# Two transformer-like blocks on one core: the x spill cut into eight pieces, and the order of the opening's chunks changed

## The reference, cut to what matters

```python
shift, scale, gate = split(silu(c) @ ada_w[l] + ada_b[l], 3)        # 2048 x 6144
shift_c, scale_c, gate_c = split(silu(c_ctx) @ ada_w[l] + ada_b[l], 3)
h  = rmsnorm(x,  norm_g[l]) * (1 + scale)   + shift
hc = rmsnorm(xc, norm_g[l]) * (1 + scale_c) + shift_c
q, k, v, up, uf, g = split_proj(h @ w_in[l])                        # 2048 x 4608
kc, vc, ...        = split_proj(hc @ w_in[l])
att = latent_attention(q, k, v, kc, vc)
x_new = x + gate * merge_branches(att, up, uf, g, ...) 
```

## Time and profile before

| | us |
|---|---|
| median of 3 runs | 2350.74 (2350.19 to 2352.19) |
| profiled execution, its own time | 2353.96 |
| its span, first to last instruction | 2352.1 |
| TensorE busy | 2271.9 (97%) |
| VectorE busy | 1297.0 (55%) |
| ScalarE busy | 1040.3 (44%) |
| GpSimd busy | 266.7 (11%) |
| moved by DMA | 437.14 MB, mean 186 GB/s |

### The profile page before, as it was taken

The page is one execution under the profiler, slowest core; times in us unless marked ns, Lnnn a source line. Parts: engine busy times, 40 slices in busy tenths (PEclk is TensorE's granted clock), DMA queues, the critical chain, the costliest instruction groups (busy, mean ns, idle before and its releaser), DMA issues.

```text
span 2352.1 us, 30034 instructions
## 1 busy us (share of the span) xinstructions
PE 2271.9 (97%) x11859; PEld 1832.5 (78%) x11859; DVE 1297.0 (55%) x2046; ACT 1040.3 (44%) x1592; POOL 266.7 (11%) x326
## 2 busy tenths in 40 slices
PE   5989999999999989999999998999999999999998
PEld 2567777777777867678888887888888888888887
DVE  3333453442432364555777776677755777567764
ACT  2222333432321255445554565555544555345553
POOL 1001100000010122100020324111100111001111
PEclk8999999999999999999999998999999999999999
DMA  9874443345655475735566544565656565666653
GB/s 357 316 277 167 147 144 110 110 142 172 224 178 179 148 273 192 238 96 159 182 208 203 176 139 152 179 197 180 188 191 194 182 186 187 197 188 187 188 190 116
DMA packets 322428, 437.14 MB, mean 186 GB/s; under 512 B 13849, under 2 KB 220113, under 8 KB 321265
## 3 DMA queue, kind: packets, MB, share of 16 engines
q1 hardware_dynamic: 316800, 413.19, 54.2%
q0 software_dynamic: 3392, 16.90, 2.0%
q10 hardware_dynamic: 2096, 5.15, 0.6%
HBM read 428.89 MB, written 6.29 MB: 185 GB/s over the span
## 4 chain that ended last, share of the span: by engine, by line
PE 85%; DVE 5%; ACT 4%; DMA 3%; issue 2%; POOL 1%; SPq 0%; ACTq 0%; POOLq 0%
PE ps L1361 24%; PE ps L1362 12%; PE ps L1336 8%; PE ps L1338 8%; PE ps L1337 8%; PE ps L1356 5%; PE ps L1358 5%; PE ps L1357 5%; PE ps L1316 3%; ACT SPL L1567 2%; DVE SPL L1818 2%; DMA RAW<-in_w_in_dram 2%; PE ps L1410 1%; PE ps L1427 1%; DMA RAW<-in_ada_w_dram 1%
## 5 line engine op out<-in xcount | busy, mean ns | idle before, releaser
L1818 DVE TENSOR_TENSOR SPL<-RAW,SPL 128x1024 fp32r<-128x1024 f32 x592 | 752.6, 1276 | 637.9 <-ACT SPL L1567 635.3
L1361 PE MATMUL ps<-HS,SPL 128*128 128x512 f32 x2688 | 959.8, 401 | 10.4 <-DVE SPL L1818 7.5
L1567 ACT ACTIVATE SPL<-RAW 128x1024 fp32r<-128x1024 f32 x592 | 621.7, 1055 | 451.2 <-PE ps L1338 174.0
L1362 PE MATMUL ps<-HS,SPL 128*128 128x256 f32 x2688 | 756.6, 281 | 0.0
L1361 PEld LDWEIGHTS ps<-HS,SPL 128*128 128x128 f32 x2688 | 507.9, 189 | 136.1 <-DVE SPL L1818 5.3
L1362 PEld LDWEIGHTS ps<-HS,SPL 128*128 128x128 f32 x2688 | 511.0, 190 | 2.0 <-issue 1.7
L1336 PE MATMUL ps<-SPL,HS 128*128 128x512 f32 x960 | 396.6, 413 | 18.7 <-DVE HS L1867 6.6
L1338 PE MATMUL ps<-SPL,HS 128*128 128x512 f32 x960 | 379.2, 395 | 0.0
L1337 PE MATMUL ps<-SPL,HS 128*128 128x512 f32 x960 | 378.7, 394 | 0.0
L1336 PEld LDWEIGHTS ps<-SPL,HS 128*128 128x128 f32 x960 | 183.2, 191 | 83.0 <-issue 28.6
L1337 PEld LDWEIGHTS ps<-SPL,HS 128*128 128x128 f32 x960 | 183.4, 191 | 41.3 <-issue 5.3
(11 more groups left out here) (289 smaller groups left out, 1691.2 us busy)
## 6 DMA issues: line engine op xcount, KB each, us to landing
RAW<-in_w_in_dram SPq DMA_DIRECT2D x208, 512.0 KB, 5.7
RAW<-in_ada_w_dram SPq DMA_DIRECT2D x192, 512.0 KB, 5.0
RAW<-in_ffn_w_up_dram SPq DMA_DIRECT2D x192, 512.0 KB, 3.6
RAW<-in_w_out_dram SPq DMA_DIRECT2D x96, 512.0 KB, 4.7
RAW<-in_ffn_w_down_dram SPq DMA_DIRECT2D x96, 512.0 KB, 4.2
x_spill<-XT POOLq DMA_DIRECT2D x2, 2048.0 KB, 15.0
XT<-x_spill POOLq DMA_DIRECT2D x1, 4096.0 KB, 16.6
MM<-in_x_dram ACTq DMA_DIRECT2D x2, 1024.0 KB, 10.8
```

The costliest lines, as they stand in the source:

```text
L1361: mm(PS[b][:, :], wr, hh, start=k == 0, stop=False, skip_group_check=True)
L1362: m = mm(PS[b][:, 256:512], wl, hh[:, 0:256], start=False, stop=k == KT - 1, skip_group_check=True)
L1567: act(SPL[:, (n - 1) % NSPL, 0, :], raw_of(i), ACT.Copy).then_inc(s_hi, 1)
L1818: tt(w[:, 1, :], raw_of(s["i"]), w[:, 0, :].bitcast(F32), ALU.subtract).then_inc(s_lo, 1)
```

## The change

- The spill goes in eight DMAs of 512 KB (`PIECES` = 4 for each half), one behind each projection chunk of units 2 and 3 (`spill_behind`); each waits for that chunk's last matmul. The waits on the spill ask for four times the count.
- kv0 moves into unit 1. Unit 1 becomes eight ada chunks, gp0, three ada, gp1, three ada, kv0, two ada. Unit 2 has kv1, kv2, kv3, gp2; unit 3 has gp3, gp4, gp5, kv4. `OPENING` is 75.
- kv4 and kv5 take three side steps for each half, six per chunk in place of two.
- `mixed` now counts the main chunks alone and puts two more ada chunks behind the 22nd and the 42nd; `FILL` falls from 6 to 4. With 61 main chunks instead of 62 behind the opening, the ada pairs stand at other places: behind kv6, gp6, the first q chunk and so on, where they stood behind kv5, kv7, gp7 and the second q chunk.

```diff
-FILL = 6
-OPENING = 74
+FILL = 4
+OPENING = 75
+PIECES = 4
...
-                    pop_side(c.group.side)
+                    pop_side(c.side)
...
-        def mixed(main, left):
+        def mixed(main, left, extra=()):
             seq = []
-            for c in main:
+            for i, c in enumerate(main):
                 seq.append(c)
-                if len(seq) % 4 == 2:
-                    seq.extend(left[:2])
-                    del left[:2]
+                if i % 2:
+                    n = 4 if i in extra else 2
+                    seq.extend(left[:n])
+                    del left[:n]
             return seq
...
+            def spill_behind(c, piece):
+                then = c.then
+
+                def f():
+                    put("spill", piece=piece, last=[multiplied()])
+                    if then:
+                        then()
+                c.then = f
...
-                    if u == 3:
-                        put("spill", last=[multiplied()])
...
-                    return cs[:8] + gp[0:1] + cs[8:12] + gp[1:2] + cs[12:]
-                beside = {0: [], 2: kv[:4], 3: gp[2:6]}[u]
+                    return cs[:8] + gp[0:1] + cs[8:11] + gp[1:2] + cs[11:14] + kv[0:1] + cs[14:]
+                beside = {0: [], 2: kv[1:4] + gp[2:3], 3: gp[3:6] + kv[4:5]}[u]
+                for i, c in enumerate(beside):
+                    spill_behind(c, 4 * (u - 2) + i)
...
-                main = [c for u in range(4) for c in start(u)], kv[4:] + gp[6:] + q0 + q1 + gf + gates
+                for c in kv[4:6]:
+                    c.side = 3
+                main = [c for u in range(4) for c in start(u)], kv[5:] + gp[6:] + q0 + q1 + gf + gates
...
-        lay_out(main0[0] + mixed(main0[1], left))
+        lay_out(main0[0] + mixed(main0[1], left, (21, 41)))
...
-                    for i, c in enumerate((4096, 0)):
-                        e.dma_start(XSP[:, c:c + 4096], XT[:, c:c + 4096]).then_inc(s_spill[i], 16)
+                    half, w = s["piece"] // PIECES, 4096 // PIECES
+                    c = 4096 * (1 - half) + w * (s["piece"] % PIECES)
+                    e.dma_start(XSP[:, c:c + w], XT[:, c:c + w]).then_inc(s_spill[half], 16)
```

More of the change, by code:

```diff
@@ L58, in __init__ @@
         self.group, self.kc, self.ap, self.shape, self.then = group, kc, ap, shape, None
+        self.side = group.side
         self.first, self.last = kc == 0, kc == (3 if shape == 4 else 7)
@@ L542, in load_tables @@
             def load_tables():
-                x["scr"] = [(s_h0, count.get("h0", 0)), (s_spill[0], 16)] if both else [(s_m2, KT), *x["ended"]]
+                x["scr"] = [(s_h0, count.get("h0", 0)), (s_spill[0], 16 * PIECES)] if both else [(s_m2, KT), *x["ended"]]
                 x["qs"] = list(x["scr"])
@@ L553, in load_dft @@
             def load_dft():
-                x["scr_a"] = [(s_h0, count["h0"])] + ([(s_spill[1], 16)] if both else x["ended"])
+                x["scr_a"] = [(s_h0, count["h0"])] + ([(s_spill[1], 16 * PIECES)] if both else x["ended"])
                 put("dft_in", l=l, last=x["scr_a"])
@@ L1290, in sync @@
             for i in range(2):
-                e.wait_ge(s_spill[i], 16)
+                e.wait_ge(s_spill[i], 16 * PIECES)
         def tensor(e):
@@ L2330, in gpsimd @@
                 elif kind == "back":
-                    for sm, v in new(*s["last"], (s_spill[0], 16), (s_spill[1], 16)):
+                    for sm, v in new(*s["last"], (s_spill[0], 16 * PIECES), (s_spill[1], 16 * PIECES)):
                         e.wait_ge(sm, v)
```

## The result

The changed kernel takes 2357.09 us in the median (2355.41 to 2361.57, ten runs) against 2351.47 before (2347.99 to 2355.12, ten runs): a ratio of 1.0026, 95% interval 1.0017 to 1.0036, so 6 us slower. 2343.5 was forecast, with a range up to 2348.5.

What follows compares the result with a forecast made beforehand. TensorE was taken as the bound, busy 2271.9 of 2352.1 us, with gaps and clock falls to win. 16.5 us removed less 9.2 added gave 7.3 won: 2346.7, or 2343.5 us for the median, range 2338.0 to 2348.5.

Steps and rivals of the forecast that it cites:

- 16.5 us removed: Waits with their clock losses gone from the opening: 8.7 us in kv6, 4.1 before kv0, 3.7 before gp2.
- terms 1 to 4: Time added up to kv7: 2.5 us before kv0, 1.3 before gp2, 2.7 at the last ada turn, 1.8 from DMAs.
- the last turn: The last ada group's turn, now ahead of kv4's first matmul: 1.9 us of waiting, 2.7 with half a clock fall.
- half a fall of the clock: Half of the 1.55 us lost to a slower TensorE clock, added behind kv0's wait and behind the last ada turn.
- 4.1 and 3.7: Gains in us from shortening the gaps before kv0 and before gp2, each counting idle time plus 1.55 of clock loss.
- terms 1 and 2: New idle time: before kv0 2.5 us (1.75 to 3.3), before gp2 1.3 us (up to 2.85).
- the pairs that move across the group boundaries: Ada pairs at new places against the groups: taken as 0, since PSUM's first banks are copied while the last fill.
- The last of the prediction's own signs of being wrong: New waits at the group boundaries between 180 and 620 us that aren't in the trace before.
- The cause of the long wait: The 6.56 us inside kv6: h's steps stand behind a late chunk's split in DVE's list, its load slowed by the spill.
- The DMAs as bound of units 2 and 3: Rival, chance 0.08: a period takes 8.9 us, seven projection chunks come 1.15 us late, clock falls behind each; 2360.6 us.
- The long wait that only moves: Rival, chance 0.14: pieces still slow the loads of kv5 to kv7, a wait like kv6's returns; 2352.1 us.
- Between the layers: First projection waits 1.3 us instead of 0.37, the next turn's load is requested up to 1.4 earlier; taken as 0.

Runs made afterwards that it cites:

- the other three with this opening: The changed kernel with its ada pairs back (2345.15 us), with the fourth pool matrix loaded first (2353.64 us), or without the extra ada chunks (2362.21 us).
- The two parts of it: The kernel before with its ada pairs shifted up to the gates alone (2358.46 us), then in the gates alone (2353.86 us).

## Why the prediction was wrong

*The opening held, in sum.* 16.5 us removed less 8.3 added (terms 1 to 4): 8.2 us were forecast up to gp6, and 10.4 came in this execution, 7.4 to 9.4 in the other three with this opening. The waits were 1.14 us before kv0 (1.75 forecast), 1.13 before gp2 (1.3), 1.73 before the last turn (1.9; 1.6 to 2.5 in the other three), 0.9 in all for late loads (1.8; 1.6 to 2.6 in the other three). I had counted half a fall of the clock twice. Behind kv0 it never fell; behind the turn it fell in two of the four executions. The 1.71 us before gp6 is 1.0 above, as forecast. But the parts of the sum are not borne out. Moving kv0 was to win 4.0 us net (4.1 and 3.7 less terms 1 and 2) and gave nothing that shows, while the six steps or the pieces alone brought gp6 to 166.4 and 169.0, as early as the whole change did. So that the sum came out right was partly luck.

*The step that failed* is the sentence on the pairs that move across the group boundaries: "I take 0 (up to 3 us if the cover of 0.9 was needed at three of them)". It cost 12 to 13 us: 13.0 in the profiled execution (14.9 less four ada chunks), 12 by the ratios (1.0026 against 0.9974 with the pairs back). I had looked at one thing only, whether PSUM's banks are copied out in time, and there it was right. But an ada pair is cover (work that hides a wait) for everything that the side steps do between two chunks, and when it has been multiplied, its slots set off a burst of loads. The runs name the places: the load of a pool matrix, asked for just behind the pair's loads (5.4 us, as the run with the matrix first shows); longer waits for turned keys and queries; attention steps; the last gate chunk, behind which no pair is left while DVE makes the first output chunk's input. The shift alone, with the old opening, costs 11.8 us. The two parts of it cost 9.4 and 4.5. About 3 us belong to the two places of four ada chunks. Which share each of the short waits up to the gates has was not tried one by one. The last of the prediction's own signs of being wrong, new waits at the group boundaries between 180 and 620 us, is what the trace shows.

*The cause of the long wait* was named rightly in the first part (h's steps behind a late split), but then I ranked the spill first among the remedies. The six steps alone remove it, with the loads as late as ever. So the pieces buy nothing that shows once the steps are in order, and they keep the DMA engines full for 58 us.

*The rivals.* The DMAs as bound of units 2 and 3 didn't come: 385 GB/s in the mean from 90 to 148, where a period at 7.75 us needs 406; the seven periods lost 0.9 us to late loads here, not 8. The Trainium skill ("DMA: Bandwidth & Descriptors", section "Specifications") puts a core's share of HBM near 358 GB/s; this trace is above it for 58 us. The long wait that only moves didn't come either. None of my rivals had its place behind kv7, though this is where the pairs of 61 main chunks change their place.

*Between the layers* I took 0 (-0.5 to +0.9). From the second layer's first projection to its ninth the changed kernel takes 64.1 us (826.6 to 890.6) instead of 66.4 (820.3 to 886.7), as the turn's 3.41 us are gone. From the first output chunk to that first projection it takes 201.7 instead of 199.9, with two ada chunks (0.9 us) fewer: 1.5 of it is the longer wait before the projection, and most of the rest the clock, at 0.76 in the 7 us behind the 2.57 us wait for the first output chunk's input (1.00 in the kernel before). Together that is 0.5 us less, so the size of the term was right. But the wait before the first projection is another than I had in mind: for DVE's `L2025`, not for the load.

## What to carry to other kernels

When an order is written out by hand, count a shift by one as a change in every place behind it: list, for each wait that isn't there today, what covers it, and ask whether the cover keeps its place. A wait that a late transfer seems to cause can be one of order: look whether what is waited for needs that transfer at all, and if not, put its steps ahead before touching the transfer. And a small load that stands in a queue behind a wait for compute can land in the burst of loads which that same compute sets free: here it took 6.51 us instead of 3.08.

## What the runs showed that I had not expected

The clock doesn't fall behind every wait, and waits of nearly the same length differ. Behind 1.13 us (gp2) and 1.73 us (the turn) the granted clock stayed at 1.00. Behind the same turn it was 0.78 and 0.77 over some 7 us in the two executions where the turn had waited 2.28 and 2.45 us. In the kernel before it was 0.76 behind the 2.16 us before gp2. Behind 2.6 to 2.7 us before the first output chunk it was 0.76 in the changed kernel and 0.77 in the kernel with the pairs shifted, but 1.00 with the gates alone shifted. Around the 4.71 us wait it was 0.91 over 20 us.

A run of ada chunks as long as the ring has slots (8) leaves 3.9 us of the next projection's load and split uncovered, where six left 0.37.
